# The state-space stage with its gathering batches of TensorE kept apart by other products

## The reference, cut to what matters

```python
u = (h @ w_in).reshape(bsz, seq, SSM_GROUPS, SSM_CH)
bu_re = jnp.einsum('bsgc,gpc->bsgp', u, bbar_re)
bu_im = jnp.einsum('bsgc,gpc->bsgp', u, bbar_im)
_, _, xs_re, xs_im = lax.associative_scan(combine, (a_re, a_im, bu_re, bu_im), axis=1)
y = (jnp.einsum('bsgp,gcp->bsgc', xs_re, c_re)
     - jnp.einsum('bsgp,gcp->bsgc', xs_im, c_im)
     + d_skip[None, None] * u)
z = jax.nn.gelu(y.reshape(bsz, seq, SSM_WIDTH))
z = z * jax.nn.sigmoid(z @ w_glu)
return z @ w_out
```

## Time and profile before

| | us |
|---|---|
| median of three runs | 2912.07 |
| profiled execution | 2911.7 |
| its span | 2909.9 |
| TensorE busy in the span | 2847.5 (98%) |
| VectorE busy in the span | 2021.8 (69%) |
| ScalarE busy in the span | 1612.0 (55%) |
| the stretch around the change, from `ada(8)` to the gate product | 83.5 to 127.4 |

### The profile page before, as it was taken

One profiled execution on the slowest core, in us unless ns is written; L12 is line 12 of the kernel. 1 busy time (PEld: TensorE's weight loads), 2 busy tenths in 40 slices (PEclk: granted clock), 3 DMA queues, 4 the chain that ended last, 5 costly groups with the idle time before them and its releaser, 6 DMA issues.

```text
span 2909.9 us, 41501 instructions
## 1 busy us (share of the span) xinstructions
PE 2847.5 (98%) x15068; PEld 2301.5 (79%) x15068; DVE 2021.8 (69%) x2243; ACT 1612.0 (55%) x1758; POOL 546.6 (19%) x479
## 2 busy tenths in 40 slices
PE   8999999998999999999999899999999999999999
PEld 4788888765788888877788688888888888888887
DVE  8742234587622326847743799999999999999998
ACT  5332323346522324445632677777777777777775
POOL 1012100113012000003100222222222222232221
PEclk9999999998999999999999999999999999999999
DMA  8422221220122322110022899999999999999995
GB/s 348 184 81 107 102 99 75 91 87 32 56 104 87 125 92 95 58 59 16 1 92 89 314 404 386 386 386 386 385 386 384 382 385 384 383 384 381 382 385 218
DMA packets 88925, 638.89 MB, mean 220 GB/s; under 512 B 10449, under 2 KB 11665, under 8 KB 26097
## 3 DMA queue, kind: packets, MB, share of 16 engines
q1 hardware_dynamic: 78592, 599.97, 52.8%
q0 software_dynamic: 9936, 36.75, 4.7%
q10 hardware_dynamic: 288, 0.65, 0.1%
HBM read 611.28 MB, written 26.05 MB: 219 GB/s over the span
## 4 chain that ended last, share of the span: by engine, by line
PE 53%; DVE 1%; ACT 0%; issue 0%; SPq 0%; DMA 0%; POOL 0%; ACTq 0%; DVEq 0%
PE banks L263 15%; PE banks L265 15%; PE banks L264 15%; PE banks L3411 1%; PE banks L3271 1%; PE banks L3393 1%; PE banks L2338 1%; PE banks L2205 1%; PE banks L2234 1%; PE banks L2361 1%; PE banks L2217 1%; DVE arena_rounded L3290 1%; PE banks L2349 0%; PE banks L3377 0%; DMA arena_rounded<-bias_dram 0%
## 5 line engine op out<-in xcount | busy, mean ns | idle before, releaser
L3290 DVE TENSOR_TENSOR arena_rounded<-arena,arena_rounded 128x2048 fp32r<-128x2048 f32 x420 | 951.0, 2286 | 89.0 <-ACT arena_rounded L3286 89.0
L3286 ACT ACTIVATE arena_rounded<-arena 128x2048 fp32r<-128x2048 f32 x420 | 801.6, 1918 | 207.5 <-PE banks L265 132.8
L263 PE MATMUL banks<-arena_rounded,operand_rounded 128*128 128x512 f32 (+1 forms) x2064 | 817.2, 396 | 2.7 <-DVE small_rounded L3582 1.3
L264 PE MATMUL banks<-arena_rounded,operand_rounded 128*128 128x512 f32 (+1 forms) x2064 | 801.6, 388 | 0.0
L265 PE MATMUL banks<-arena_rounded,operand_rounded 128*128 128x512 f32 (+1 forms) x1504 | 583.1, 388 | 0.0
L263 PEld LDWEIGHTS banks<-arena_rounded,operand_rounded 128*128 128x128 f32 x2064 | 387.8, 188 | 82.5 <-issue 2.9
L264 PEld LDWEIGHTS banks<-arena_rounded,operand_rounded 128*128 128x128 f32 x2064 | 388.2, 188 | 76.7 <-issue 1.0
L265 PEld LDWEIGHTS banks<-arena_rounded,operand_rounded 128*128 128x128 f32 x1504 | 282.4, 188 | 58.8
L263 PE MATMUL banks<-operand_rounded,arena_rounded 128*128 128x512 f32 (+1 forms) x728 | 272.9, 375 | 0.1
L265 PE MATMUL banks<-operand_rounded,arena_rounded 128*128 128x512 f32 (+1 forms) x728 | 270.5, 372 | 0.0
L264 PE MATMUL banks<-operand_rounded,arena_rounded 128*128 128x512 f32 (+1 forms) x728 | 270.3, 371 | 0.0
(11 more groups left out here) (525 smaller groups left out, 3856.6 us busy)
## 6 DMA issues: line engine op xcount, KB each, us to landing
arena<-in_gate SPq DMA_DIRECT2D x140, 1024.0 KB, 7.7
arena<-in_up SPq DMA_DIRECT2D x140, 1024.0 KB, 7.8
arena<-in_down SPq DMA_DIRECT2D x140, 1024.0 KB, 6.0
arena<-in_dense SPq DMA_DIRECT2D x62, 2048.0 KB, 7.8
arena<-in_dense SPq DMA_DIRECT2D x6, 1024.0 KB, 4.9
small<-in_rows SPq DMA_DIRECT2D x7, 512.0 KB, 8.0
resid<-in_x SPq DMA_DIRECT2D x4, 512.0 KB, 8.3
expert_sums<-operand SPq DMA_DIRECT2D x4, 512.0 KB, 4.4
```

What stands on the lines that cost most here:

```text
L263: nc.tensor.matmul(out, left[0], right[0], start=start, stop=False)
L264: nc.tensor.matmul(out, left[0], right[1], start=False, stop=False)
L3286: nc.scalar.activation(high[q % NHI], raw[:, q, :], ACT.Copy).then_inc(high_ready, 1)
L3290: nc.vector.tensor_tensor(low[q], raw[:, q, :], high[q % NHI].bitcast(F32), ALU.subtract).then_inc(low_ready, 1)
```

## The change

The order of TensorE's calls is altered, and `tapped` can be told to do only part of its eight products. `ada(9)` moves from before `gather(0)` to after it. `tapped(3)` is cut into its first two products, which go before `gather(2)`, and its other six, which go between `gather(2)` and `gather(3)`. `from_states(1)` moves behind `tapped(2)`. The wait of `tapped` for `tap_kept` is issued by both of its parts. No product is added or removed, and no other engine's program changes.

```diff
-            def tapped(i):
+            def tapped(i, part=range(RUN)):
                 pe.wait_ge(tap_kept, 4 * i + 4)
-                for d in range(RUN):
+                for d in part:
                     nc.tensor.matmul(y_runs[:, i, :, d:RUN], taps[:, i, d, :], in_runs[:, i, :, 0:RUN - d],
                                      start=(d == 0), stop=False)
 
@@ -893,21 +893,22 @@
             tapped(1)
             turn(3)
             ada(8)
-            ada(9)
             pe.wait_ge(g_kept_act, 8)
             pe.wait_ge(g_kept_dve, 8)
             gather(0)
+            ada(9)
             gather(1)
             ada(10)
+            tapped(3, range(2))
             pe.wait_ge(run_read, 4)
             gather(2)
+            tapped(3, range(2, RUN))
             gather(3)
-            tapped(3)
             ada(11)
             from_states(0)
-            from_states(1)
             pe.wait_ge(ada_copied, 1)
             tapped(2)
+            from_states(1)
             pe.wait_ge(run_read, 8)
```

## The result

The changed kernel takes 2916.64 us (median of 22 runs, 2913.14 to 2922.04), the kernel before 2912.36 in the same comparison (22 runs, 2909.96 to 2919.55). The forecast was 2917.0. The profiled execution took 2916.0 with a span of 2914.1, 4.2 above that of before.

A forecast was written before the change was run, and what follows sets the result against it. TensorE, busy for 98% of the span, was taken to bound the kernel. The terms 0 + 3.7 + 0.3 + 1.1 gave 5.1 us more, 2917.2 on the median, rounded 2917; range for 8 in 10: 2912.5 to 2920.

The forecast's parts named there:

- 1: `ada(9)` after `gather(0)`: block still comes at 91.5, so gap in `gather(1)` and low clock stay; saves 0, bounds 0 to 2.8.
- 2: `tapped(3)` before `gather(3)`: adds 4.22 us to the way to VectorE's half 1, zero over TensorE alone.
- 3: Late instruction block 21 records into `gather(3)`, held until the third weight load ends: 0 to 0.9 us, taken as 0.3.
- the 2.4 us that the prediction allows: Time from the start of an instruction block's transfer to TensorE having it, taken from the first gap: 93.93 - 91.5.
- Rival B: Block for `gather(3)` comes at 109.5, TensorE idles 0.9 us there and the clock falls: 6.3 to 8.0 us, 2919; chance 0.17.
- 4: `tapped(2)` before `from_states(1)`: costs nothing, as `from_states(0)` covers ScalarE's copy until 115.6, a cover of 1 us.
- 5: Affine rows come 4.2 us later, at 131.1; TensorE waits 3.4 us at their transpose; 3.7 us more after the slack.
- the slack of 0.49: What the chain from `gather(3)` to VectorE's affine rows, 19.1 us long, has to spare before TensorE takes them up, in us.
- 6: Low clock among the first gate products after the wait for the affine rows: bounds 0 and 3.4 us, taken as 1.1.
- rival A: Block request slips ahead of the load, so gap in `gather(1)` and low clock go: +0.9 to +2.6 us, 2914; chance 0.18.

The follow-up runs named there:

- e2: Kernel before with only the two parts of `tapped(3)` moved ahead of `gather(2)` and `gather(3)`: median 2918.96 us, ratio 1.0009 to 1.0029.
- e7: Kernel before with 64 further wait instructions at the start of TensorE's program, to move the instruction block borders: median 2916.05 us, ratio 0.9995 to 1.0018.
- e8: Kernel before with the weight loads after `ada(8)`, `ada(9)` and `ada(10)` each cut into four DMAs: median 2928.22 us, ratio 1.0031 to 1.0066.
- b1: Kernel before, unchanged, as a run of its own: median 2912.94 us over 12 runs, ratio 0.9980 to 1.0013.
- b2: Kernel before, unchanged, run once more for one profile: 2911.58 us.
- b3: Kernel before, unchanged, a further single profile: 2923.59 us.
- e1: Kernel before with only `ada(9)` moved between `gather(0)` and `gather(1)`: median 2918.05 us, ratio 1.0001 to 1.0021.
- e3: Changed kernel with `tapped(3)` back in one piece behind `gather(3)`: median 2921.62 us, ratio to before 1.0005 to 1.0030.
- e4: Changed kernel with VectorE making the affine rows before the low part of the first output weight chunk: median 2912.58 us, ratio to before 0.9975 to 0.9999.
- e5: Changed kernel with the transpose of the affine rows behind the first quarter of the gate product: median 2912.88 us, ratio to before 0.9987 to 1.0010.
- e9: Changed kernel with the changes of e4 and e5 together: median 2912.41 us, ratio to before 0.9985 to 1.0008.
- e10: e9 with `from_states(0)` and `from_states(1)` together again ahead of `tapped(2)`: median 2912.51 us, ratio to before 0.9984 to 1.0006.

## Why the prediction was right

The time came within 0.4 us of the 2917.0, by a mechanism that was half right and by errors that cancelled. That the number was so close is luck. By its points:

1. Wrong. The prediction took 0, with the block at 91.5 again. It was there at 90.5 to 90.6, 1.0 us earlier, and that was enough:

```profile
q8 instruction: 1, 0.02, 57.8%
```

(the DMA of 90.5 to 90.6 of the changed kernel). The two gathering batches took (89.07 - 85.10) + (95.30 - 90.92) = 8.35 us and not 96.47 - 87.06 = 9.41, and the low clock did not come: 1.06 + (3.44 - 1.85) = 2.65 saved, against a bound of 2.8. This is no chance of one profile: all seven profiles with `ada(9)` ahead of `gather(0)` (before, e2, e7, e8, b1, b2, b3) have a gap of 0.98 us or more in `gather(1)` and a low clock in `ada(10)`, and all seven with it behind (changed, e1, e3, e4, e5, e9, e10) have at most 0.5 us and `ada(10)` at 1.92. The failed step is the reading that a block asked for during a load waits for that load's end. It is delayed by the load, but it started before the end, 4.3 us after the load's first packets at 86.2 where it had started 5.1 us after them. The 1.8 us by which the request was said to come earlier don't fit the prediction's own count either: 53 records into `gather(0)` is 88.6 in the kernel before, 69 records into it is 87.2 in the changed one, so it came 1.5 us earlier, if a block is asked for at the border one block ahead. The block's start kept 1.0 of that. Another thing changed with it, which no run separates: when the block started, at 90.5, only the first load was out, as `ada(9)` ended at 91.0 and the second waits for it, where in the kernel before two were. The Trainium skill, "Runtime: NRT & Kernel Launch", section "Instruction fetch mechanics", says that fetching is mostly hidden; the gaps show that it was not, in either kernel, but the outcome that I had tied to it, the loss of the gap, did come.

2. Right: the taps put 4.4 us ahead of `gather(3)` (4.22 said; cut in two they take 1.81 + 2.60, from the starts of the rows above). e2, in which only they move, has the wait of 3.37 that was forecast.

3. Zero, not 0.3. `gather(3)` takes 4.04 like the others. The border in it was reached at 105.53 + 21 x 0.030 = 106.2, and its block starts between 103.6 and 103.8, again amid a load and not at the load's end:

```profile
q8 instruction: 1, 0.02, 30.8%
```

With the 2.4 us that the prediction allows from there, it was there at 106.0 to 106.2, just in time. Rival B was that close; it was the same failed step as in point 1 that kept it away.

4. It cost nothing, as said, for as long as the wait covers it: two gaps of 0.55 and 1.74 where one of 1.04 was, both before the affine rows. In e10, without the cover, the same part is worth 1.03 us of the stage.

5. Right in kind: VectorE's half 1 starts 26.45 us after `ada(8)` and not 24.37, and the gate product 1.64 later. 2.08 less the slack of 0.49 is 1.59. The chain from that start to the last affine row is 18.97 us long in both kernels. The wait was 1.88 and not 3.4, because of what point 1 saved. e4 takes it away and e5 makes it shorter, each in another way, and they gave back 4.1 and 3.8 us of the 4.3 in the medians, 3.46 and 2.27 in the stage. That settles the place.

6. Mis-sized: 1.1 said, 2.65 measured, near the upper bound of 3.4. The loss can be read from the window as well, (1 - 0.81) x 14.56 = 2.8. The low clock lasted 6.8 us, twice as long as the shortest stretches of the earlier trace rows, and the gate product ran into 5.7 of it. The prediction looked at the wait alone, and did not have the gaps of 0.55 and 1.74 us so close before it. The gaps alone did no harm: in e4 and e9, with both gaps and no wait, no low clock came.

In all: 0 became -2.65, 0.3 became 0, 3.7 became 4.25 (4.41, and 0.33 more where batches join, less the slack of 0.49), 1.1 became 2.65: 4.25 us for 5.1. The mechanism was rival A's, with more low clock behind it than A had (2.65, and not 0 to 1.7). B's place, a gap in `gather(3)`, did not appear in the changed kernel. It did in e1 and e3, where the batches touch; that I did not foresee.

## What to carry to other kernels

Dense batches of small products, at 15 and 30 ns a record here, can outrun the arrival of their instructions: count the records between gaps that are put down to "issue", and if they are multiples of 128 (256 instructions, as each record has its weight load), try other, longer products between the batches. But ask of each product put in front who waits behind it: here it was 4.4 us on the one chain that had 0.5 us of slack, and its cure was a new place for what the chain ends in, the affine rows in VectorE's order (e4) or the transpose in TensorE's (e5). After a delay is taken away, look at the next border: e1 and e3 lost there more than they had gained.

## What the runs showed that I had not expected

A batch of products on 32 rows can be 100% busy and yet stay at 1.2 GHz: in b3 the granted clock was 0.50 over 13.86 us without a gap, where in the kernel before it was 1.00 over the same records. The low clock of b3 began at the gap in `gather(1)`. In e1, e3 and b3 the full clock came back behind the second pair, within the taps (128 rows, 512 to 64 columns): at 114.8, 115.5 and 121.1 us (e3's clock, 0.50 from 105.5 to 115.5, and b3's, 0.50 to 116.1 and into the 6.74 us of its taps, show it in the rows above). In the profiles of this case every return between 83 and 130 us lies within an `ada` or a `tapped` or at most 1.4 us behind one, and none deep in a gathering batch; but in b3 `ada(10)` went by without it. What decides it is open. How often the kernel before goes this way differs between the comparisons, 1 of 22 executions above 2917 in the first and 13 of 35 in that of e1 to e4; why is open, and of the long executions only b3 has a profile.

Cutting the loads of 2 MB in four took them from 373 to 224 GB/s, and raised TensorE's wait for the instruction block among them from 1.2 to 5.4 us.
